# Two gated attentions and their output projections in one block each, with the projection's first two tiles started among the last heads

## What is computed

```python
# gla_mixer: scores, o_intra and o_inter by chunks of 64, then
    o = (o_intra + o_inter).reshape(bsz, seqlen, H, DV)
    o = rms_norm(o, norm_w) * jax.nn.silu(g.reshape(bsz, seqlen, H, DV))
# ssd_gla_layer
    return jnp.concatenate([y_ssd, y_gla], axis=-1) @ w_out
# second_block
        o_hg = hgrn2_mix(hq.astype(f32), hf.astype(f32), hi.astype(f32), lbs[l])
        o_hg = (head_rms(o_hg).reshape(B, S, HG_HEADS * HG_DV) * hg_norm_w[l].astype(f32)
                * jax.nn.silu(hg.astype(f32)))
        y_hg = o_hg.astype(x.dtype) @ w_branch_hg[l]
```

## Time and profile before

| | before |
|---|---|
| median of 3 runs | 3623.99 us |
| lowest and highest | 3622.63 and 3625.62 us |
| the profiled execution | 3625.65 us |
| its span in the profile | 3623.8 us |
| PE busy in the span | 3523.6 us (97%) |
| DVE, ACT, POOL busy | 2035.3, 1401.7, 1659.9 us |
| mean granted PE clock | 0.993 of full speed |

### The profile page before, as it was taken

The page is one execution under the profiler, slowest core; times in us unless marked ns, Lnnn a source line. Parts: engine busy times, 40 slices in busy tenths (PEclk is TensorE's granted clock), DMA queues, the critical chain, the costliest instruction groups (busy, mean ns, idle before and its releaser), DMA issues. The chain is left out here.

```text
span 3623.8 us, 49877 instructions
## 1 busy us (share of the span) xinstructions
PE 3523.6 (97%) x17281; PEld 2964.5 (82%) x17281; DVE 2035.3 (56%) x3579; ACT 1401.7 (39%) x2171; POOL 1659.9 (46%) x828
## 2 busy tenths in 40 slices
PE   8899899999999999999899999999999999999999
PEld 6667688887678888878687788789999999888887
DVE  7825234403654440158335241559899992788887
ACT  3332432225653222222311332333349994333333
POOL 5343364445115444431443444436777776344321
PEclk9999999999999999999999999999999999999999
DMA  5122133222003322320232133335879997999997
GB/s 178 36 91 82 53 107 96 95 96 98 24 30 110 93 96 95 92 81 24 73 107 70 60 92 98 105 105 175 259 222 342 380 380 278 370 361 362 361 361 265
DMA packets 275171, 580.23 MB, mean 160 GB/s; under 512 B 119713, under 2 KB 153889, under 8 KB 273617
## 3 DMA queue, kind: packets, MB, share of 16 engines
q1 hardware_dynamic: 238160, 444.07, 37.5%
q0 software_dynamic: 36864, 134.23, 10.4%
HBM read 523.66 MB, written 54.56 MB: 160 GB/s over the span
## 5 line engine op out<-in xcount | busy, mean ns | idle before, releaser
L756 POOL TENSOR_TENSOR w_lo<-ring,w_hi 128x1024 fp32r<-128x1024 f32 (+1 forms) x159 | 412.1, 2592 | 578.2 <-ACT w_hi L708 578.1
L566 PE MATMUL ps<-h_hi,w_hi 128*128 128x512 f32 x1384 | 541.1, 391 | 2.3 <-DVEq L850 1.2
L567 PE MATMUL ps<-h_lo,w_hi 128*128 128x512 f32 x1384 | 539.5, 390 | 0.0
L3937 POOL TENSOR_TENSOR w_lo<-ring,w_hi 128x1024 fp32r<-128x1024 f32 x142 | 359.1, 2534 | 147.3 <-ACT w_hi L3798 145.3
L708 ACT CAST w_hi<-ring 128x1024 fp32r<-128x1024 f32 (+1 forms) x159 | 176.9, 1113 | 594.6 <-PE ps L570 569.6
L3988 PE MATMUL ps<-h_hi,w_hi 128*128 128x384 f32 (+1 forms) x1152 | 398.5, 346 | 3.8 <-DVE h_lo L482 3.1
L3798 ACT CAST w_hi<-ring 128x1024 fp32r<-128x1024 f32 x270 | 282.9, 1048 | 299.6 <-PE ps L559 168.2
L3989 PE MATMUL ps<-h_lo,w_hi 128*128 128x384 f32 (+1 forms) x1152 | 393.7, 342 | 0.0
L570 PE MATMUL ps<-h_hi,w_lo 128*128 128x512 f32 x1384 | 341.8, 389 | 0.0
L3941 POOL DMA_INDIRECT xT<-in_expert_v,row_index x128 | 186.8, 1460 | 327.3 <-DVE ps L4236 312.0
L2468 POOL TENSOR_TENSOR w_lo<-ring,w_hi 128x1024 fp32r<-128x1024 f32 x84 | 209.4, 2494 | 220.0 <-ACT w_hi L2437 219.9
(11 more groups left out here) (489 smaller groups left out, 7512.4 us busy)
## 6 DMA issues: line engine op xcount, KB each, us to landing
ring<-in_expert_u SPq DMA_DIRECT2D x128, 512.0 KB
ring<-in_expert_v SPq DMA_DIRECT2D x128, 512.0 KB
ring<-in_w_gate_up SPq DMA_DIRECT2D x88, 512.0 KB
acts<-expert_gelu SPq DMA_DIRECT2D x128, 192.0 KB
gates<-peer_region SPq DMA_DIRECT2D x48, 512.0 KB
peer_region<-acts SPq DMA_DIRECT2D x128, 192.0 KB
peer_region<-gates SPq DMA_DIRECT2D x128, 192.0 KB
ring<-in_w_down SPq DMA_DIRECT2D x32, 704.0 KB
```

The lines of the kernel that those rows point to most:

```text
L566: pe.matmul(out, w_hi[:, at], x_hi(k), start=start and k == 0, stop=False)
L567: pe.matmul(out, w_hi[:, at], x_lo(k), start=False, stop=False)
L756: pool.tensor_tensor(half(c.w_lo, s), raw(s), half(c.w_hi, s).bitcast(F32), ALU.subtract).then_inc(c.lo_done.sem, 1)
L3937: pool.tensor_tensor(at_slot(c.w_lo, i), at_slot(c.ring, i), at_slot(c.w_hi, i).bitcast(F32), ALU.subtract).then_inc(c.lo_done.sem, 1)
```

## The change

Both attentions get a block that also holds the projection behind them, so the barrier between goes. `linear` gets `begun`: its first two output tiles are no longer its own. A new class holds their steps, and the attentions call these by hand at chosen places.

```diff
+class FirstTiles:
+    def __init__(self, c, fill, weight, src, rs, hi, lo, by_pool, later):
...
+    def normal(self, dve, k):
+        dve.scalar_tensor_tensor(self.src(k), self.src(k), self.weight(k), self.rs(k), ALU.mult, ALU.mult
+    def high(self, act, k):
+        act.wait_ge(self.made.sem, self.made.at(k + 1))
+        act.copy(self.hi(k), self.src(k)).then_inc(self.cut.sem, 1)
+    def low(self, engine, k):
+        engine.wait_ge(self.cut.sem, self.cut.at(k + 1))
+        engine.tensor_tensor(self.lo(k), self.src(k), self.hi(k).bitcast(F32), ALU.subtract
+    def products(self, pe, k, tiles=(0, 1)):
...
+        for m in tiles:
+            if k == 0:
+                pe.wait_ge(c.lo_done.sem, c.lo_done.at(fill.nb + 5 + m))
+            mm = passes(pe, c.ps[:, m, :], fill.slot(c.w_hi, m)[:, at], fill.slot(c.w_lo, m)[:, at],
+                        self.hi(k), self.lo(k), k == 0, k == DT - 1)
+    def rest(self, pe):
+        for m in range(2):
+            for k in self.later:
+                self.products(pe, k, (m,))
```

Both GLA and HG now split the next projection's two first pieces (`low_both`). In `linear_block`, PE calls `begun.rest` (k = 6 and 7) and starts its own pieces at 2. In HG:

```diff
+        TURN, STATE, OUT, SUM = [5] * (H - 1) + [3], [7] * (H - 1) + [4], [5] * (H - 1) + [6], [7] * (H - 1) + [2]
@@ PE: in the last pair of heads the sums of the pair before come one level earlier; at the end
                 outputs(H - 2)
                 outputs(H - 1)
+                pe.wait_ge(kept.sem, kept.at(MASKED * H))
+                first.products(pe, 0)
                 sum_squares(H - 2)
+                first.products(pe, 1)
                 sum_squares(H - 1)
+                for h in range(2, H - 2):
+                    first.products(pe, h)
@@ DVE: one normal among the last decays, the others behind the last states
+                            if (h, l) == (H - 2, LV - 1):
+                                normal(0)
@@ POOL
                 gated_head(5)
-                fill.low_then(pool)
+                fill.low_both(pool)
                 gated_head(6)
                 gated_head(7)
-                pool.wait_ge(gated.sem, gated.at(H))
+                first.low(pool, 3)
+                first.low(pool, 5)
```

In GLA the first pairs' roots are made before head 2's outputs are kept, and four normalised tiles with their splits go ahead of head 3:

```diff
@@ PE, head 3 (H - 1)
                     states(h, beside_states)
+                    if h == H - 1:
+                        sum_squares(H - 2)
+                        pe.wait_ge(kept.sem, kept.at(2 * H))
+                        first.products(pe, 0, (0,))
+                        first.products(pe, 1, (0,))
                     outputs(h)
...
+                first.products(pe, 2, (0,))
+                first.products(pe, 3, (0,))
                 sum_squares(H - 1)
+                for k in range(4):
+                    first.products(pe, k, (1,))
+                for k in range(4, 6):
+                    first.products(pe, k)
@@ DVE: EVICT moves gate tile 7 to head 3, behind the new work of head 2
-                EVICT = (((), (0,), (1,)), ((2,), (), (3, 4)), ((5,), (), (6, 7)), ((), (), ()))
+                EVICT = (((), (0,), (1,)), ((2,), (), (3, 4)), ((5,), (), (6,)), ((7,), (), ()))
+                    if h == H - 2:
+                        for k in range(4):
+                            normal(k)
+                            if k:
+                                first.low(dve, k - 1)
+                        first.low(dve, 3)
```

More of the change, by code:

```diff
@@ L575, in linear @@
            width=D, more=None, ends=None, loads=(), rest=0, whole=None, run=None, head=True, tail=True, tokens_next=False,
-           makes=None, takes=None, scaled=False, bank0=0, ahead=0, given=None, squares=None, both=False):
+           makes=None, takes=None, scaled=False, bank0=0, ahead=0, given=None, squares=None, both=False,
+           begun=None):
     with ExitStack() as ctx:
@@ L585, in linear @@
                      Normal(c, ctx, normal, width, whole, ends, (hi, lo)) if normal else None, more, loads, rest,
-                     run, head, tail, tokens_next, makes, takes, scaled, bank0, ahead, given, squares, both)
+                     run, head, tail, tokens_next, makes, takes, scaled, bank0, ahead, given, squares, both, begun)
 def opened(c, run):
@@ L594, in linear_block @@
 def linear_block(c, ctx, w, kt, nb, hi, lo, dst, add, src, then, beside, root_of, normal, more, extra=(), rest=0,
-                 run=None, head=True, tail=True, tokens_next=False, makes=None, takes=None, scaled=False, bank0=0, ahead=0, given=None, squares=None, both=False):
+                 run=None, head=True, tail=True, tokens_next=False, makes=None, takes=None, scaled=False, bank0=0, ahead=0, given=None, squares=None, both=False,
+           begun=None):
     np_ = 1 if kt <= DT else 2
@@ L836, in _ @@
                 one(1, 1, 0, 1, 1, second=True)
-            pieces(one, None if root_of or makes or more or given else pe.Fori, 2 if takes else 1 if src or normal else 0)
+            if begun:
+                begun.rest(pe)
+            pieces(one, None if root_of or makes or more or given else pe.Fori,
+                   2 if takes or begun else 1 if src or normal else 0)
             if rest:
@@ L1048, in close @@
         c.bank_free.close(self.nb + 2)
-        c.started = (2, 1)
+        c.started = (2, 2) if both else (2, 1)
     def slot(self, t, m):
@@ L1560, in scaled, with forget_attention @@
     return program
-def forget_attention(c, q, k, F, v, out, roots, gate, masks, masks_loaded, fill):
+def forget_attention(c, q, k, F, v, out, roots, gate, masks, masks_loaded, fill, first, block):
     nc = c.nc
@@ L2004, in close, with direct_attention @@
         self.c.spend(12, self.carried)
-def direct_attention(c, x, v, out, gate, roots, fill):
+def direct_attention(c, x, v, out, gate, roots, fill, first, block):
     nc = c.nc
```

246 lines of the change are left out of this document (173 added, 73 removed).

## The result

The changed kernel takes 3600.2 us (median of four, 3597.7 to 3601.6), the kernel before 3623.5 in the same session: a ratio of 0.9933, 95% interval 0.992 to 0.9946. That is 23.3 us less, inside the predicted range of 3588 to 3604, but 7 us above the predicted 3593. The profiled execution took 3600.15 us, its span 3598.4 (before 3623.8), with 3518.3 us of PE busy (98%) and a mean granted clock of 0.992.

A forecast was written before the change was run, and what follows sets the result against it. TensorE, busy 97% of the span, was taken as the bound, with time to win where it waits or runs slowly. GLA's 17.4 plus HG's 14.2 made 31.6 us, less 0.6 given back: 3593 us, range 3588 to 3604.

The forecast's parts named there:

- GLA: From GLA's last states TensorE works without stall, reaching the projection's third tile 18.8 us later: 17.4 us gained.
- The tight place: In GLA, DVE evicts gate tile 7 just before TensorE needs its bank for head 2's sum: 0.5 us spare.
- HG, ScalarE's order: In HG, ScalarE's logarithm, exponential and cast precede the turns, ending at 1728.5; states of head 6 move to 1729.1.
- HG, POOL beside DVE: In HG, POOL's gating and two w_lo may delay DVE's last decays: 0 to 2.1 us, taken as 1.0.
- the point from which DVE is late: In HG, DVE's last masked copy could end as late as 1729.7 before delaying the states' evictions.
- the main case: Whole kernel: both projections start earlier as worked out, 3589 to 3598 us, chance 0.71.
- The 0.6 given back: Both places: 0.6 us allowed for two jumps into the projections' code and for semaphores left out of the handovers.
- DVE bound in both places: Rival: DVE's queue limits GLA and HG, with a product each 1.9 us in HG; 3602 us, chance 0.17.
- No overlap: Rival: both projections' products still wait for the last roots, only the second tile fills gaps; 3612 us, chance 0.06.
- slower by the clock: Rival: low clock over more than 6 of the projections' 12 remaining tiles makes the kernel slower; chance 0.03.
- a sign of being wrong: In the windows over the changed stretches, a granted clock well below 1 would show the prediction wrong.
- The other sign named for HG: In HG, the states of head 6 would come about 1.5 us later against DVE's last decays.

The follow-up runs named there:

- hg_pool_after: The changed kernel with both of POOL's w_lo in HG waiting for DVE's last masked copy: 3595.0 us.
- the control: The changed kernel measured again without any edit, in a later session: 3596.3 us.
- hg_occupy: hg_pool_after with three matmuls of no use (384 columns, float32) added in TensorE's last waits of HG: 3591.6 us.

## Why the prediction was right, and where it was off

**GLA: right, step by step.** States to third tile 18.81 against 18.8; gain 17.46 against 17.4. With the 1.36 us taken off by which the whole stage ran late, head 2's output starts on ScalarE at 405.9 (406.0 forecast), the fourth low part ends at 406.7 (406.7) and low part 7 at 422.0 (421.9). POOL held DVE once, and the low part took 2.75. The tight place, DVE's eviction of gate tile 7:

```profile
408.52 0.69 DVE L1128 TENSOR_TENSOR proj_gla<-ps,root 128x512 f32<-128x512 f32 x1 [0.48 <-PE ps L1106]
```

It ended at 409.21, and TensorE came to the sum at 409.61: 0.4 us to spare against 0.5 forecast.

**HG, ScalarE's order: right, but hidden.** In the changed kernel the cast of the first normalised tile ended at 1714.72, which is 1728.4 on the clock of before (13.72 added), 1728.5 forecast. With POOL out of the way the states of head 6 came 24.50 us after the turn of head 4, which is 1728.9, 1729.1 forecast. That chain would have set the time.

**HG, POOL beside DVE: the step that failed.** The prediction took 1.0 us, "the middle, since both rows exist", of ends 0 and 2.1. The states came 3.56 us later than with the `w_lo` out of the way. Two things in that term were wrong. First, the choice: the middle stood for neither case. The low part of DVE in the earlier trace rows ended behind POOL's `w_lo` of the earlier trace rows, and here POOL had three long instructions in a row; DVE waited out each of them, and the pair of decays took 3.97 to 3.99 us in every profile of a kernel that left the first `w_lo` there. The worst case was worked out almost rightly: last masked copy over at 1731.8, measured 1717.96 + 0.72 + 13.72 = 1732.4. Second, the point from which DVE is late: the prediction took 1729.7, by the states' evictions, but TensorE's turns wait for the decays (2.22 and 0.45 us in the timeline), and the states stand behind the second turn in TensorE's order. Against `hg_pool_after` DVE's last masked copy ended 4.25 us later and the states came 3.56 later, so 0.7 was hidden, where the prediction had 1.7 (1728 to 1729.7). By the Trainium skill (SBUF — State Buffer, section Who interferes with whom) as the prediction used it, with POOL first each time, HG's gain was to be 13.1; the measured 11.1 is 2.0 below even that: 0.9 by this point of lateness, 0.6 by the later end, and the rest by HG's other terms (next paragraph).

**HG, what the net price was.** Of the 3.56 us the third tile lost 1.94, because the low clock lay partly over waiting in place of work. With both the hold and the low clock away the gain is 58.88 - 44.10 = 14.8, against 15.2 worked out ahead of the lock term. The wait at k = 4 was 0.39 (0.6 forecast), and states to third tile 19.7 (19).

**The sum: 7.2 us off.** The result lies in the range, but above the main case (3589 to 3598); the control's 3596.3 is inside it. Of the 7.2 us, 3.1 are HG's, 3.1 were lost outside the changed parts, and 1.7 what the prediction took off for the median, since this time the profiled execution lay at the median. The 0.6 given back went the other way.

**The 0.6 given back.** The two jumps showed no such cost: the distances contain them, and GLA's came out at the bare sum. What was lost instead was 3.1 us net by the clock outside the changed parts, and no term stood for it. It isn't bound to the change: the control had the same code and got most of it back. The median of before less the two distances is 3623.5 - 28.5 = 3595.0; the control's median is 3596.3, the first session's 3600.2.

**Rivals and signs.** DVE bound in both places: only half, since GLA was untouched and HG's k = 2 to 7 ran with one wait of 0.39; its time of 3602 came near the measured one for another reason. Its pace of 1.9 us for a product was also too slow, since the stretch from 422.8 us that it divides begins with the three L313; the eight products themselves start within 11.1 us (425.88 to 436.96), 1.6 apart. No overlap, and slower by the clock: neither. The clock did fall in the new stretch (0.62 from 1713 to 1722), which the prediction had named as a sign of being wrong, but it was back before the projection's products, and none of the tiles of either projection lost time to it. The other sign named for HG, states some 1.5 us later against the last decays, didn't come either: they start 0.03 us behind DVE's last masked copy (0.44 before), since the decays were what was late.

## To carry to other kernels

Where GpSimd has long instructions queued one behind another beside a chain of short VectorE instructions with two inputs in SBUF, count each of its instructions at full length onto the chain as the bad case, not a middle value; move them beside instructions that read PSUM. Find the first consumer of the delayed queue before granting it slack, and ask what the clock does in the waits that remain: removing a wait can move the low clock onto work. Judge a part of a few microseconds by a distance inside the trace, and not by medians, which moved by 4: the distances repeated to 0.05 us here, but for one of five in HG, in which the clock stayed low longer (0.87).

## What the runs showed of the hardware

- In HG's tail VectorE and GpSimd take turns: beside a gating and two `w_lo` back to back, DVE got through with one instruction in each gap and waited the next out, 1.49 us for the first decay, then until 1713.7 and until 1715.9. POOL lost little, 5.01 us for the two `w_lo`, against 4.66 with DVE out of its way.
- GpSimd can be the one that pays. At 318.20 us in the kernel before, the first of the two `w_lo` took 5.01 us, while VectorE's `tensor_tensor` instructions from SBUF ran one behind another at their usual 0.41 and 0.68 us until 320.97, with no turn for GpSimd. At the same place in the changed kernel, `w_lo` came at 319.51 and took 2.54, and one of VectorE's took 2.61. So a chain without a gap may keep GpSimd out; what decides in each case no run shows.
- The lock spares evictions. In `hg_pool_after` the states' evictions (0.29, and 0.73 for two) ran at their usual length inside the two `w_lo`, which took 4.66. The Trainium skill states it as a rule, that a VectorE instruction with at most one input in SBUF, outside the two-port modes, doesn't contend with GpSimd (SBUF — State Buffer, section Who interferes with whom); the trace agrees, for an eviction that adds a scaled SBUF tile to PSUM.
- The granted clock fell in HG's tail in all eight profiles in which the changed HG had its waits there (0.4 to 3.0 us each), and in none of the three in which they were filled or two of them gone. In `hg_pool_after` the fall cost 1.8 us, by `hg_occupy`.
